# The first modulation products on TensorE instead of VectorE and GpSimd, with x normalised ahead of them

## The reference, cut to what matters

```python
mod   = silu(c) @ w_mod + b_mod                # c: 1024 numbers, w_mod: 1024 x 6144
mod_c = silu(c_ctx)[None, :] @ w_mod + b_mod   # the same weights, a second vector
sh1, sc1, g1, sh2, sc2, g2 = split(mod, 6)     # of mod_c only sh1c and sc1c are used
h  = rms_norm(x, norm1_w)   * (1 + sc1)  + sh1
hc = rms_norm(ctx, norm1_w) * (1 + sc1c) + sh1c
p, pc = h @ w_in, hc @ w_in   # mLSTM keys, queries, values, gates; attention q, k, v; ...
```

## Time and profile before

| | before |
|---|---|
| median of three runs | 1544.36 us (1543.13 to 1547.33) |
| profiled execution, first to last instruction (its own time; the page has no other) | 1541.6 us |
| TensorE busy | 1372.9 us, 89% |
| VectorE, ScalarE, GpSimd busy | 928.6, 644.2, 711.9 us (60, 42, 46%) |
| mean granted TensorE clock | 0.921 |

### The profile page before, as it was taken

The page is one execution under the profiler, slowest core; times in us unless marked ns, Lnnn a source line. Parts: engine busy times, 40 slices in busy tenths (PEclk is TensorE's granted clock), DMA queues, the critical chain, the costliest instruction groups (busy, mean ns, idle before and its releaser), DMA issues. The chain is left out here.

```text
span 1541.6 us, 25613 instructions
## 1 busy us (share of the span) xinstructions
PE 1372.9 (89%) x9454; PEld 1242.2 (81%) x9454; DVE 928.6 (60%) x1452; ACT 644.2 (42%) x1068; POOL 711.9 (46%) x295
## 2 busy tenths in 40 slices
PE   2189989999998998999979899889999799699997
PEld 1068868867676898999968667889999799699997
DVE  5970025377766347676752555167777678677776
ACT  4333233222222446555544233355555444454552
POOL 7545452220112784555547410335655378455552
PEclk9589999979878999999989967899999999899999
DMA  7433341113544453554535310224545355255452
GB/s 286 150 99 120 98 135 56 55 41 100 167 144 162 136 181 110 180 187 175 200 114 173 107 44 1 71 94 173 195 175 193 112 162 165 82 185 183 163 182 77
DMA packets 57731, 209.38 MB, mean 136 GB/s; under 512 B 6448, under 2 KB 7472, under 8 KB 57280
## 3 DMA queue, kind: packets, MB, share of 16 engines
q1 hardware_dynamic: 57168, 206.59, 39.7%
q0 software_dynamic: 496, 1.87, 0.3%
HBM read 207.39 MB, written 1.05 MB: 135 GB/s over the span
## 5 line engine op out<-in xcount | busy, mean ns | idle before, releaser
L283 POOL TENSOR_TENSOR wlo<-raw,whi 128x1024 fp32r<-128x1024 f32 x272 | 666.4, 2465 | 790.6 <-ACT whi L955 790.5
L422 PE MATMUL ps<-Hh,whi 128*128 128x256 f32 (+2 forms) x1912 | 568.7, 297 | 66.5 <-DVE Hl L1406 49.5
L423 PE MATMUL ps<-Hl,whi 128*128 128x256 f32 (+2 forms) x1912 | 558.0, 292 | 0.0
L424 PE MATMUL ps<-Hh,wlo 128*128 128x256 f32 (+2 forms) x1912 | 557.4, 292 | 0.0
L422 PEld LDWEIGHTS ps<-Hh,whi 128*128 128x128 f32 (+1 forms) x1912 | 376.4, 197 | 90.8 <-issue 52.8
L955 ACT ACTIVATE whi<-raw 128x1024 fp32r<-128x1024 f32 x338 | 351.9, 1049 | 100.8 <-PE ps L453 40.6
L423 PEld LDWEIGHTS ps<-Hl,whi 128*128 128x128 f32 (+1 forms) x1912 | 377.4, 197 | 2.4
L424 PEld LDWEIGHTS ps<-Hh,wlo 128*128 128x128 f32 (+1 forms) x1912 | 376.8, 197 | 3.0
L422 PE MATMUL ps<-dh,whi 128*128 128x256 f32 x656 | 190.7, 291 | 31.5 <-DVE wlo L1692 17.5
L1717 DVE SCALAR_TENSOR_TENSOR arena<-ps,sm,arena 128x255 f32<-128x255 f32 (+1 forms) x264 | 127.4, 483 | 103.0 <-ACT arena L1195 95.9
L423 PE MATMUL ps<-dl,whi 128*128 128x256 f32 x656 | 188.3, 287 | 0.0
(11 more groups left out here) (285 smaller groups left out, 1644.9 us busy)
## 6 DMA issues: line engine op xcount, KB each, us to landing
raw<-in_stream SPq DMA_DIRECT2D x386, 512.0 KB, 3.7
X<-in_xc SPq DMA_DIRECT2D x2, 1024.0 KB, 13.7
arena<-in_crow SPq DMA_DIRECT2D x1, 1024.0 KB, 5.2
out_y<-X SPq DMA_DIRECT2D x8, 128.0 KB, 2.0
kx<-in_const POOLq DMA_DIRECT2D x1, 512.0 KB, 12.1
arena<-in_wgate POOLq DMA_DIRECT2D x1, 400.0 KB, 8.8
params<-in_params POOLq DMA_DIRECT2D x1, 372.0 KB, 7.6
k<-in_const POOLq DMA_DIRECT2D x1, 256.0 KB, 6.6
```

The costliest lines, as they stand in the source:

```text
L283: pool.tensor_tensor(wlo[:, slot, :], raw[:, rslot, :], whi[:, slot, :].bitcast(f32), ALU.subtract).then_inc(rest_done[0], 1)
L422: pe.matmul(out, lh, rh, start=start, stop=False, skip_group_check=True)
L423: pe.matmul(out, lh, rl, start=False, stop=False, skip_group_check=True)
L424: return pe.matmul(out, ll, rh, start=False, stop=stop, skip_group_check=True)
```

## The change

The first 16 modulation blocks are stored by inputs: block 2k + s has 128 inputs (chunk k) on its partitions and 1024 outputs along them (s = 0 shift, 1 scale). silu(c) and silu(c_ctx) come as columns, `c_cols[:, k, 0:2]`, in a stationary matrix of 32 columns whose other 30 are zero. Each block takes two float32 matmuls of 512 columns; the four halves (shift or scale, first or second) accumulate over k in four groups of 32 partitions of PSUM bank 7. TensorE adds the square-sum matmul behind block 8: VectorE sums the eight squares first, so one matmul is left of eight. While the blocks come, VectorE makes the reciprocal root and normalises X into `sq`. At the end VectorE copies bank 7, TensorE transposes it in four, and VectorE adds the bias and forms the scale.

The h units become: VectorE scales and shifts from `sq` into PSUM bank 5, ScalarE scales, shifts and rounds from `sq` into `Hh`, VectorE subtracts into `Hl`. TensorE makes, for each chunk, the gates' three matmuls and those of key blocks 0 and 1, side by side in banks 2, 0 and 1. The 1 MB broadcast of c is gone; c arrives as 16 numbers on each partition, and as two small rows for later (GpSimd's queue). GpSimd loads `KX` only when block 8 has been used. SP's loads of X have a semaphore each. The square sums of the later blocks and their norms are as before.

The diff, cut to its core:

```diff
+            sp.dma_start(c_raw, ccol_d).then_inc(s_ccol, 16)
-            sp.dma_start(ar(A_MO, 2 * D), crow_d.broadcast_to((P, 2 * D))).then_inc(s_crow, 16)
...
                     if kind == "mod":
-                        sp.wait_ge(mod_done, mod_count(n, False))
                         if n < MOD_FIRST:
-                            sp.wait_ge(mod_mul, mod_count(n, True))
+                            sp.wait_ge(mod_used, n + 1)
+                        else:
+                            sp.wait_ge(mod_done, n - MOD_FIRST + 1)
...
         def _(pool):
+            pool.memset(c_cols, 0.0).then_inc(S["c_clear"], 1)
             pool.dma_start(K0[:, :], const_d).then_inc(s_k0, 16)
             pool.dma_start(PR[:, :], params_d).then_inc(s_par, 16)
             pool.dma_start(ar(A_KT, KC * GATE_P), wgate_d).then_inc(s_wg, 16)
+            for half in range(2):
+                pool.dma_start(c_kept[half], crow_d[:, 512 * half:512 * half + 512]).then_inc(s_crow, 16)
+            pool.wait_ge(mod_used, 9)
             pool.dma_start(KX[:, :], const1_d).then_inc(s_kx, 16)
...
-            for i, n in enumerate(mine):
-                r = RAW_OF_MOD[n]
-                wait_raw(pool, r)
-                if i >= 2:
-                    pool.wait_ge(S["mod_acc"], i - 1)
-                pool.tensor_tensor(modj_p[i % 2], raw[:, r % RING, :], cB[1], ALU.mult).then_inc(mod_mul, 1)
...
-            pe.wait_ge(s_k0, 16)
-            sumsq(0)
+            pe.wait_ge(S["silu_c"], 1)
+            for n in range(MOD_FIRST):
+                k, s = divmod(n, 2)
+                r = RAW_OF_MOD[n]
+                wait_raw(pe, r)
+                for half in range(2):
+                    j = 2 * s + half
+                    mm = pe.matmul(PS[32 * j:32 * j + 32, 7, :], c_cols[:, k, :],
+                                   raw[:, r % RING, 512 * half:512 * half + 512], start=k == 0, stop=k == KC - 1)
+                mm.then_inc(mod_used, 1)
+                if n == 8:
+                    pe.wait_ge(s_k0, 16)
+                    pe.wait_ge(S["sq_sum"], KC - 1)
+                    pe.matmul(PS[:, 1, :], ones, sq[:, 0, :], start=True, stop=True).then_inc(S["ss_ready"], 1)
+            pe.wait_ge(S["mod_copy"], 1)
+            for c in range(4):
+                mm = pe.transpose(PS[:, 6, P * c:P * c + P], mod_rows[:, P * c:P * c + P], ident)
+            mm.then_inc(S["mod_t"], 1)
 
             pe.wait_ge(S["wg_lo"], 1)
+            for q in range(2):
+                wait_rest(pe, q)
             for k in range(KC):
                 pe.wait_ge(S["hl_done"], 2 * k + 2)
                 mm = mm3(PS[0:GATE_P, 2, :], wgh[:, k, :], wgl[:, k, :], Hh[:, k, :], Hl[:, k, :],
                          k == 0, k == KC - 1)
-            mm.then_inc(S["gates_ps"], 1)
+                if k == KC - 1:
+                    mm.then_inc(S["gates_ps"], 1)
+                for q in range(2):
+                    mm = mm3(PS[:, q, :], *w(q, k), Hh[:, k, :], Hl[:, k, :], k == 0, k == KC - 1)
+                    if k == KC - 1:
+                        mm.then_inc(blk_done, 1)
...
-            for q in range(28):
+            for q in range(2, 28):
                 gp_job(q)
...
+            act.wait_ge(s_ccol, 16)
+            act.wait_ge(S["c_clear"], 1)
+            act.activation(c_cols[:, :, 0:2], c_raw.rearrange("p (k v) -> p k v", v=2), ACT.Silu)\
+               .then_inc(S["silu_c"], 1)
+            act.wait_ge(s_crow, 32)
+            for half in range(2):
+                act.activation(c_kept[half], c_kept[half], ACT.Silu).then_inc(S["c_kept"], 1)
...
             rsqrt_start(0)
-            for k in range(5, KC):
-                mod_sum(k)
+            splits_upto(1)
             act.wait_ge(S["mod_ready"], 1)
             for u in range(2 * KC):
-                norm_hi(0, u, MOD[:, u // 2, 0, u % 2:u % 2 + 1])
-                if u % 3 == 2:
-                    splits_upto(u // 3)
+                k, v = divmod(u, 2)
+                if v == 0:
+                    act.wait_ge(S["x_unit"], k + 1)
+                act.activation(Hh[:, k, v * T:v * T + T], sq[:, k, v * T:v * T + T], ACT.Identity,
+                               bias=MOD[:, k, 0, v:v + 1], scale=SC[:, u:u + 1]).then_inc(S["hh_done"], 1)
+                if u % 4 == 3 and u < 15:
+                    splits_upto(2 + u // 4)
...
+            def mod_finish():
+
+                dve.wait_ge(mod_used, MOD_FIRST)
+                dve.tensor_copy(mod_rows, PS[:, 7, :]).then_inc(S["mod_copy"], 1)
+                dve.wait_ge(S["mod_t"], 1)
...
+            def first_norm():
+
+                for k in range(1, KC):
+                    dve.wait_ge(S["sq_ready"], k + 1)
+                    if k >= 2:
+                        dve.wait_ge(S["sq_sum"], k - 1)
+                    dve.tensor_tensor(sq[:, 0, :], sq[:, 0, :], sq[:, k, :], ALU.add).then_inc(S["sq_sum"], 1)
+                dve.wait_ge(S["ss_ready"], 1)
+                newton(n_v, n_y, n_t, n_r, PS[:, 1, :], 1.0 / D, S["newton"],
+                       lambda x: dve.wait_ge(S["y0_done"], x))
+                dve.wait_ge(S["newton"], 1)
+                for k in range(KC):
+                    dve.tensor_tensor(sq[:, k, :], X[:, k, :], n_r, ALU.mult).then_inc(S["x_unit"], 1)
+                dve.wait_ge(s_par, 16)
+                mod_finish()
+                for u in range(2 * KC + 1):
+                    if u < 2 * KC:
+                        k, v = divmod(u, 2)
+                        if v == 0:
+                            dve.wait_ge(S["x_unit"], k + 1)
+                        if u >= 2:
+                            dve.wait_ge(S["hl_done"], u - 1)
+                        dve.tensor_scalar(PS[:, 5, T * (u % 2):T * (u % 2) + T], sq[:, k, v * T:v * T + T],
+                                          SC[:, u:u + 1], MOD[:, k, 0, v:v + 1], ALU.mult, ALU.add)\
+                           .then_inc(S["h32_done"], 1)
+                    if u >= 1:
+                        k, v = divmod(u - 1, 2)
+                        dve.wait_ge(S["hh_done"], u)
+                        dve.wait_ge(S["h32_done"], u)
+                        dve.tensor_tensor(Hl[:, k, v * T:v * T + T], PS[:, 5, T * ((u - 1) % 2):T * ((u - 1) % 2) + T],
+                                          Hh[:, k, v * T:v * T + T].bitcast(f32), ALU.subtract)\
+                           .then_inc(S["hl_done"], 1)
```

More of the change, by code:

```diff
@@ L42 @@
 RAW_OF_MOD = {n: r for r, (kind, n) in enumerate(STREAM) if kind == "mod"}
[L45 to L56, removed]
 FFN_STARTS = (S_FFN1, S_FFN2, S_FFN3)
@@ L180, in build @@
         dens = SM[:, 288:292]
-        cB = [ar(A_MO, D), ar(A_MO + D, D)]
+        c_raw = ar(A_MO, 2 * KC)
+        c_cols = ar(A_MO + 2 * KC, 32 * KC).rearrange("p (k v) -> p k v", v=32)
+        mod_rows = ar(A_MO + 512, 512)
         c_kept = [ROWS[64:65, 0:512], NG[64:65, :, :].rearrange("p a t -> p (a t)")]
         c_lat = ar(A_QT, D)
-        modj_v, modj_p = [ar(at, D) for at in (A_AK, A_AQ, A_AQ + D)], [ar(A_QT, D), ar(A_AV, D)]
         ROWJ = sb("junk", [P, T], mybir.dt.bfloat16)
@@ L252, in _ @@
             for half in range(2):
-                sp.dma_start(X[:, 4 * half:4 * half + 4, :], xc_d[:, 4 * half:4 * half + 4, :]).then_inc(s_x, 16)
+                sp.dma_start(X[:, 4 * half:4 * half + 4, :], xc_d[:, 4 * half:4 * half + 4, :])\
+                  .then_inc(s_x[half], 16)
             r = 2
@@ L972, in squares @@
                     if n == 0:
-                        act.wait_ge(s_x, 32)
+                        if k % 4 == 0:
+                            act.wait_ge(s_x[k // 4], 16)
                     else:
@@ L995, in norm_hi @@
                     act.activation(out, h32[:, u % 4, :], ACT.Identity, bias=shift).then_inc(S["hh_done"], 1)
-            def mod_sum(k):
-                for n in (2 * k, 2 * k + 1):
-                    if mod_by_gpsimd(n, 1):
-                        i = mod_count(n, True) - 1
-                        act.wait_ge(mod_mul, i + 1)
-                        act.activation(modj_p[i % 2], modj_p[i % 2], ACT.Copy, accum_out=MOD[:, k, n % 2, 1:2])\
-                           .then_inc(S["mod_acc"], 1)
             act.preload_act_table_set("natural_log_exp_and_others")
-            mod_sum(0)
-            mod_sum(1)
             squares(0)
-            for k in range(2, 5):
-                mod_sum(k)
             act.wait_ge(s_wg, 16)
@@ L1370, in newton @@
                 dve.scalar_tensor_tensor(r, t, 1.5, y, ALU.add, ALU.mult).then_inc(ready, 1)
-            def norm(n, scale, shift=None):
-                width, bank = (2 * T if n == 0 else T), ss_bank(n)
-                units = 2 * KC if n == 0 else KC
-                if n == 0:
-                    for k in range(KC):
-                        mod_products(k)
-                    dve.wait_ge(s_par, 16)
+            def first_norm():
[29 more added lines that the diff above has]
+                           .then_inc(S["hl_done"], 1)
@@ L1387, in chunk @@
```

(17 more changed lines are left out.)

64 lines of the change are left out of this document (21 added, 43 removed).

## The result

The changed kernel takes 1498.03 us in the median of four runs (1495.12 to 1500.24), the kernel before, on the same chip, 1545.62 (1543.13 to 1547.33): ratio 0.9687 [0.9642, 0.9731]. The forecast was 1501.8, and the range held the time. The profiled execution spans 1494.9 us, 46.7 less than the one before. Of that, 39.1 us are there when key block 2 leaves PSUM; the forecast put 42.6 ahead of that point and nothing behind it.

A forecast was written before the change was run, and what follows sets the result against it. The prediction took VectorE to bound the head up to 62.37 us and TensorE the tail. Key block 1 leaving PSUM at 61.6 instead of 104.2 gains 42.6 us: 1544.4 - 42.6 = 1501.8 us, range 1490 to 1514.

The forecast's parts named there:

- Step 1: Modulation loads: block 2 lands at 14.9 us, later blocks at 1.27 us each, ending about 32.7 with the held constants.
- Step 2: TensorE's modulation products: 1.71 us a block one after the other, slow pace charged to block 2, ending at 41.4 us.
- rival A: Modulation products: column groups overlap, matmuls end at 33.3 to 34, gain 45.9 us, total 1498.5; chance 0.30.
- Step 3: Work beside the modulation products, charged nothing: x normalised at 38.1 us, 3.3 ahead of 41.4; second remainder 41.6, wanted 45.2.
- Step 4: Behind the modulation products: bank copy, four transposes, two adds and the scale take 2.2 us, ending at 43.6.
- Step 5: h units, gates and two key blocks: TensorE starts at 45.2 us, 72 products at 0.228 take 16.4, ending at 61.6.
- rival B: h units: GpSimd stretches the PSUM form, TensorE ends 5.6 us later at 67.2, total 1507.4; chance 0.10.
- Step 6: Gate chain behind the keys: 17 us, done at 77.2, still hidden before ScalarE's stop at block 6, 81.2; margin 4.
- by one constant: Sign for the tail: from key block 1's copy out of PSUM at 61.6 us on, every instruction is earlier by one constant.
- C: Modulation stage: slow TensorE pace stays throughout, keys end at 83.7 us, gain 20.5, total 1523.9; chance 0.08.
- D: 72 products and beyond: half clock carried on, keys end at 98 us; until 125 it gives 1551.6, slower; chance 0.03.
- E: Tail: products were not the bound, or an order elsewhere gives the gain back; 1544 us; chance 0.02.

The follow-up runs named there:

- e10: Changed kernel with ScalarE's copies of key blocks 0 and 1 ahead of the gate functions and the second constants behind the second remainder, another chip: ratio 0.9736 to before.
- e3: Changed kernel with all modulation products in output columns 0 to 31, four accumulators in four banks and three more copies: 1512.96 us, ratio 0.9794.
- e5: Changed kernel with VectorE's scaling in the h units going to SBUF instead of PSUM bank 5: 1500.67, 1501.32, 1523.77 and 1526.12 us, ratio 0.979.
- e1: Changed kernel with ScalarE's copies of key blocks 0 and 1 ahead of the gate-addition wait, split 5 and gate functions: 1491.03 us, ratio 0.9648.
- e2: Changed kernel with side by side undone, all gate products first, then the key blocks one behind the other: 1500.44 us, ratio 0.9705.
- e0: The changed kernel again with no edit: 1498.89 us, ratio 0.9725.
- e4: The kernel before the change once more, unedited, one traced execution: 1558.69 us.
- e7: Changed kernel with both key copies ahead of the gate functions and the second constants late: one execution 1494.53 us, three 1509.7 to 1510.8, median 1510.21.
- e9: Changed kernel with only the copies of key blocks 0 and 1 ahead of split 5 and gate functions, on another chip: ratio 0.9743 to before.

## Why the prediction was right, and where it was not

**Step 1, the loads: right.** Block 2 at 15.3 (said 14.9), then 1.28 us a block (1.27), the constants in between.

**Step 2, the products: wrong, and rival A right.** The failed step is "I take 1.71, the nearest row". Column groups overlap (at most 0.52 us for a block right behind another), so the stream paces the stage, and the last product ended at 34.3 where the forecast said 41.4 and A 33.3 to 34. Even the lower end of the bounds, 0.85, was too high: it counted the two halves of one block, but a shift block and the scale block behind it lie in different groups too. Of the 7.1 us between forecast and measured, 1.7 are the slow pace charged to block 2, which fell on blocks 0 and 1 alone here; and in e10, where the granted clock stood at 0.50 from 12.1 to 18.8 us, blocks 2 to 4 began 1.28 us apart all the same. e3 priced the serial form: 1.71 and 43.1. The rule cited there, the Trainium skill's TensorE: Matmul & The Clock Gate, Packing small matmuls, agrees with this trace, and deserved more than 0.30: the serial rows it was weighed against had no column groups in them at all.

**Step 3, the cover: right with little to spare.** The c rows let ScalarE go at 12.14, x was normalised at 33.87, 0.4 us ahead of the last product; under the serial forecast it would have had 7.5.

**Step 4, the finish: mis-sized.** 2.2 us forecast, 3.7 measured (34.3 to 38.0). The term is "the scale at 0.19", measured 1.74 under GpSimd's remainder. It cost next to nothing: key block 1's remainder, which A named, came within 0.04 us of the same start.

**Step 5, h, gates and keys: the mechanism right, earlier by A.** TensorE started at 40.54 (A 39.8, though A's own terms, 35 + 1.05 + 2 x 2.4, make 40.9) at half clock until 43.6, then 0.228 us a product, and ended at 58.85 (A 58.3, forecast 61.6). No VectorE operation of the h units took over 0.55 us, so rival B was false; e5 shows that the danger was real and that the PSUM form is what averts it.

**Step 6, behind: the step that failed.** It followed ScalarE's wait for the gate chain and found it hidden, which it was: 76.83 against block 6 at 84.65. It did not ask who reads the key blocks out, and behind what. "If every wait behind the second key block is unchanged" was the assumption, and one was new. It cost 3.27 us of pause and about 3.0 of half clock; with the 0.55 by which the keys ended later than in A, that is the 6.8 us between A's 63.7 for key block 2 (109.64 less 45.9) and 70.58. e1 removed it and got 5.2 back; e2 shows that it cancelled the side by side order.

**The sum: right with two errors that cancel.** Against the forecast, the head gained 3.5 us too little: 39.06 for 42.6. The tail gained 7.6 in this execution (4.3 in e0), where nothing was forecast. The last FFN, from its table load to the end, by stretch, before and after:

```profile
1339.39:1541.60 202.21, 190.42 (x1552) 188.06 (x1551) 146.52 (x234) 95.87 (x150) 98.01 (x40) 0.98 0.43 151
```
```profile
1298.10:1494.90 196.80, 186.68 (x1552) 186.10 (x1550) 142.72 (x234) 95.90 (x150) 99.97 (x40) 0.99 0.43 155
```

The same 1552 matmuls take 5.4 us less, at nearly the same clock. All ten traces of kernels with the column groups show 196.8 to 196.9, the two of before 202.2 and 200.9, e3 200.15. So it goes with the kernel rather than with the execution. The traces show where it sits: in that FFN TensorE waits for a remainder on VectorE (L1692, L1700 after) nine times in the first trace of before, seven times in e4, five in e3 and twice in the kernel after and six further traces of kernels with the column groups. Why VectorE is late more often is open: no run changed something in the tail alone. The other 2.2 us are the attention stage (4.2, a matter of the execution, by e4) less what other stages lost. A's 1498.5 hit the 1498.03 by the same luck: too much in the head, nothing in the tail.

**Rivals C, D and E: false.** The pace doubled behind block 1 of the modulation stage and within the first ten of the 72 products, as the earlier trace rows had it, and from key block 2 on the table loads kept 39 us or more. But they are not earlier "by one constant", as the prediction's signs had it: the gain runs from 39.1 to 46.7 us.

## What to carry to other kernels

When a stage is moved ahead, list who frees each buffer that the next stage takes, and what stands ahead of that instruction on its engine: here a copy of 0.6 us, queued behind four others, undid a reordering worth 5 us, partly through the clock that fell in the pause. Small matmuls whose outputs lie in different groups of 32 partitions are to be priced as overlapping, not by the nearest serial row. And beside a busy GpSimd, an intermediate in PSUM can be cheaper than one in SBUF though the operation itself is slower (0.55 against 0.41 us).

## What the runs showed of the hardware that was not expected

**A longer time at half clock.** In the second attention stage every trace has 44.4 us at half clock. In most, 10.2 more come some 30 us later. In e4 and e7 the clock is back at full for 3.4 us and then falls to half for 54.6. By stretch (the clock is the third number from the end), e9 and e7:

```profile
880.00:900.00 20.00, 18.74 (x78) 14.67 (x78) 10.20 (x23) 6.31 (x15) 0.00 (x0) 0.67 0.00 1
900.00:920.00 20.00, 19.93 (x125) 15.09 (x124) 9.02 (x27) 6.70 (x27) 0.00 (x0) 1.00 0.00 1
```
```profile
880.00:900.00 20.00, 18.82 (x72) 15.12 (x72) 10.50 (x22) 5.61 (x12) 0.00 (x0) 0.59 0.01 1
900.00:920.00 20.00, 20.00 (x70) 14.93 (x71) 5.47 (x16) 4.09 (x16) 0.00 (x0) 0.50 0.00 1
```

In the same 20 us, e9 does 125 matmuls and e7 70. e4 shows it for the kernel before (69 from 940 to 960 us, where the first trace of before has 115). In those 3.4 us of e7 TensorE stands for 1.2 us (between 895 and 897), but so it does in e9 (between 894 and 896), where the clock stays up. The other executions have no trace that shows it. By times some 15 to 25 us above the rest of their kernel, with a lower mean clock, it came in 1 of 13 executions of the changed kernel and its controls, in 5 of the 25 of before beside the experiments, in 3 of 10 with the copies first alone, in 10 of 16 with the constants late, in 1 of 4 of e2, in 2 of 4 of e5 and in none of 4 of e3. That it is more frequent with the constants late may be chance; e9 and e10, on one chip in the same rounds, both had three of six. What decides it is open.

**One chip's median is not the next one's.** The copies first took 1491.03 in the median on one chip and 1501.70 on another, with a head that was if anything shorter (key block 2 out at 65.38 and 64.20): whether it beats the changed kernel depends on that half clock, and only the 6 us in the lower group are shown.
